# The last layer's residual kept in blocked feature order, beside its normed rows

## The reference

```python
h = rms_norm(x, g_norm1) * (1.0 + sc1) + sh1
...
mix = jnp.concatenate([attn, conv], axis=-1) @ w_out
x = x + gt1 * mix

h2 = rms_norm(x, g_norm2) * (1.0 + sc2) + sh2
x = x + gt2 * hier_moe(h2, ...)          # 32 experts, each token goes to 2 of them
return rms_norm(x, g_final)

# one expert on its rows
(silu(rows @ w_gate[e]) * (rows @ w_up[e])) @ w_down[e]
# w_gate, w_up: 1024 x 512 each, w_down: 512 x 1024; 2 MB each
```

## Time and profile before

| | |
|---|---|
| median of 3 runs | 1577.19 us (1577.14 to 1578.6) |
| the profiled execution's own time | 1580.41 us |
| its span (first to last instruction) | 1578.6 us |
| PE matmul busy | 1398.5 us, 89% |
| DVE busy | 680.4 us, 43% |
| ACT busy | 354.6 us, 22% |
| POOL busy | 110.9 us, 7% |
| moved by DMA | 338.08 MB, mean 214 GB/s |
| mean granted TensorE clock | 0.959 |

### The profile page before, as it was taken

One profiled execution on the slowest core, in us unless ns is written; L12 is line 12 of the kernel. 1 busy time (PEld: TensorE's weight loads), 2 busy tenths in 40 slices (PEclk: granted clock), 3 DMA queues, 4 the chain that ended last, 5 costly groups with the idle time before them and its releaser, 6 DMA issues.

```text
span 1578.6 us, 17570 instructions
## 1 busy us (share of the span) xinstructions
PE 1398.5 (89%) x6706; PEld 706.5 (45%) x6706; DVE 680.4 (43%) x1259; ACT 354.6 (22%) x776; POOL 110.9 (7%) x227
## 2 busy tenths in 40 slices
PE   4999999999999899999899978979996977868784
PEld 2444444555464444664644445455442333323331
DVE  4674114884366623322499775263121112111125
ACT  2434104562220243431400063110000000000001
POOL 3000000010100000001100000112000000000012
PEclk9999999999999999999999989989997989989896
DMA  9763315004276541003424123169999999999993
GB/s 340 277 222 107 103 57 125 2 1 160 91 254 218 184 160 54 1 1 107 152 88 160 54 107 158 57 235 393 413 414 412 415 415 417 413 414 419 416 395 157
DMA packets 97421, 338.08 MB, mean 214 GB/s; under 512 B 10343, under 2 KB 16280, under 8 KB 88760
## 3 DMA queue, kind: packets, MB, share of 16 engines
q1 hardware_dynamic: 83040, 307.24, 50.7%
q0 software_dynamic: 5664, 13.70, 3.1%
q10 hardware_dynamic: 8632, 15.99, 2.8%
HBM read 323.34 MB, written 17.24 MB: 216 GB/s over the span
## 4 chain that ended last, share of the span: by engine, by line
PE 65%; DMA 17%; DVE 11%; issue 3%; ACT 2%; SPq 1%; POOL 1%; DVEq 0%; ACTq 0%; POOLq 0%
PE bank L707 16%; PE score_banks L699 14%; DMA slots<-in_w_exp_up 12%; PE score_banks L1139 8%; PE bank L1166 4%; PE bank L881 3%; PE bank L683 3%; PE score_banks L707 2%; PE score_banks L1153 2%; DMA slots<-in_w_mod 2%; PE bank L981 2%; PE score_banks L972 2%; DVE bufD L1922 2%; PE score_banks L893 1%; DVE slots L1922 1%
## 5 line engine op out<-in xcount | busy, mean ns | idle before, releaser
L707 PE MATMUL bank<-slots 128*128 128x512 f32 x608 | 264.8, 593 | 2.6 <-PE bank L707 1.2
L699 PE MATMUL score_banks<-slots 128*128 128x512 f32 (+1 forms) x584 | 245.1, 578 | 6.6 <-ACTq L1298 4.0
L1139 PE MATMUL score_banks<-slots,norm_row 128*64 128x512 f32 (+1 forms) x672 | 151.2, 623 | 41.9 <-DMA slots<-in_w_exp_up 41.6
L707 PEld LDWEIGHTS bank<-slots 128*128 128x128 f32 x608 | 114.1, 190 | 144.8 <-issue 143.6
L699 PEld LDWEIGHTS score_banks<-slots 128*128 128x128 f32 x584 | 112.0, 194 | 132.9 <-issue 129.8
L2375 DVE TENSOR_TENSOR mix<-probsT,score_banks 128x256 f32<-128x256 f32 (+1 forms) x39 | 14.4, 370 | 290.2 <-ACT probsT L1586 290.0
L1166 PE MATMUL bank<-slots,mix 128*64 128x512 f32 (+1 forms) x864 | 116.9, 486 | 11.8 <-issue 9.9
L1586 ACT ACTIVATE probsT<-score_banks 128x256 f32<-128x256 f32 (+1 forms) x39 | 13.4, 342 | 446.2 <-PE score_banks L1139 387.4
L1139 PEld LDWEIGHTS score_banks<-slots,norm_row 128*64 128x64 f32 (+1 forms) x672 | 51.8, 146 | 135.6 <-issue 135.0
L707 PE MATMUL score_banks<-slots 128*128 128x512 f32 (+1 forms) x256 | 97.0, 534 | 0.3 <-PE score_banks L707 0.3
L1139 PE MATMUL score_banks<-slots,mix 128*32 128x256 f32 x896 | 61.7, 436 | 25.3 <-DMA slots<-in_w_exp_up 25.3
(11 more groups left out here) (345 smaller groups left out, 1636.8 us busy)
## 6 DMA issues: line engine op xcount, KB each, us to landing
slots<-in_w_exp_down SPq DMA_DIRECT2D x32, 2048.0 KB
slots<-in_w_exp_gate SPq DMA_DIRECT2D x32, 2048.0 KB, 28.6
slots<-in_w_exp_up SPq DMA_DIRECT2D x32, 2048.0 KB
slots<-in_w_in SPq DMA_DIRECT2D x16, 2048.0 KB, 8.7
slots<-in_w_mod SPq DMA_DIRECT2D x24, 1024.0 KB, 5.2
slots<-in_ada_w SPq DMA_DIRECT2D x18, 1024.0 KB, 6.3
slots<-in_w_out SPq DMA_DIRECT2D x6, 2048.0 KB, 7.8
slots<-in_ada_w SPq DMA_DIRECT2D x3, 2048.0 KB, 20.2
```

The lines of the kernel that those rows point to most:

```text
L699: last = mm(bank[:, cols], w[:, k, lo:lo + P], src[:, k, cols], start=(k == 0), stop=(k == kts - 1))
L707: last = mm(bank[:, 0:cols], src[:, k, t * P:(t + 1) * P], rhs(k), start=(k == 0), stop=(k == kts - 1))
L1139: last = mm(out, rows[:, k, :], e_gu[it.p][:, :, k, c * pc.ff:(c + 1) * pc.ff], start=(k == 0), stop=(k == KT - 1))
```

## The change

The last layer's residual leaves `x`. When the last gated result is added, the sum is written to `bufC`, in blocks (`residual(t)` is tile t of it, `by_block` reads natural order as blocks). The normed rows now go to `x`, so both sides of the norm are contiguous. Everything behind works on the residual in `bufC`: the transposes for the router, the squares, the additions of results, and the last norm, which writes `bufA` back in natural order.

`pick_rows` still multiplies `C_tok` by `onehot`. Since `C_tok` now holds the residual before the norm, `onehot` is multiplied by 1/rms of each token first. The store of the normed rows reads `x`. The third set's down matrix (experts 3, 6, 9, ...) goes to `x`, and so do the results gathered into `gathered[0]`. Nothing but the store reads the normed rows in `x`, so SP's wait for `rows_picked` goes.

```diff
+        def by_block(row):
+            return row.rearrange("p (q k) -> p k q", k=KT)
+        def residual(t, half=slice(0, D // KT)):
+            return bufC[:, t * D:(t + 1) * D].rearrange("p (k q) -> p k q", k=KT)[:, :, half]
...
-        e_down.append(bufC.rearrange("p (k n) -> p k n", k=FT))
+        e_down.append(x[:, :, :])
...
-        gathered = [tok(bufC), hT.rearrange("p b n -> p (b n)").rearrange("p (t n) -> p t n", t=TT)]
+        gathered = [x[:, :, :], hT.rearrange("p b n -> p (b n)").rearrange("p (t n) -> p t n", t=TT)]
...
-            return j % SUMS // 2, slice(j % 2 * W, (j % 2 + 1) * W)
+            return j % SUMS // 2, slice(j % 2 * W // KT, (j % 2 + 1) * W // KT)
...
-            sp.dma_start(xs.rearrange("(t p) d -> p t d", p=P), C_tok).then_inc(xs_out, 16)
+            sp.dma_start(xs.rearrange("(t p) d -> p t d", p=P), x[:, :, :]).then_inc(xs_out, 16)
             sp.wait_ge(logitsT_ready, 2)
             load_ahead(2, 1)
-            sp.wait_ge(rows_picked, 2)
             sp.wait_ge(xs_out, 16)
             load_ahead(2, 2)
...
-                    transposes(tr_banks, tr_filled, [every_8th(x[:, t, :], k + j) for j in range(4)])
+                    transposes(tr_banks, tr_filled, [C_tok[:, t, (k + j) * P:(k + j + 1) * P] for j in range(4)])
...
-                fn(bufC[:, t * D:(t + 1) * D], x[:, t, :], ACT.Square, accum_out=ss[:, t:t + 1]).then_inc(squares_ready, 1)
+                fn(x[:, t, :], C_tok[:, t, :], ACT.Square, accum_out=ss[:, t:t + 1]).then_inc(squares_ready, 1)
...
-                v.tensor_tensor(onehot.rearrange("p t (e s) -> p t e s", e=PICKED),
+                chain(v.tensor_tensor(onehot.rearrange("p t (e s) -> p t e s", e=PICKED),
...
+                v.tensor_tensor(onehot, onehot, ss[:, 0:TT].unsqueeze(2).to_broadcast([P, TT, PICKED * WIDE]), ALU.mult)\
+                    .then_inc(onehot_ready, 1)
...
-                rows, out = x[:, t, :], C_tok[:, t, :]
-                if by_expert_block:
-                    rows, out = rows.rearrange("p (q k) -> p k q", k=KT), out.rearrange("p (k q) -> p k q", k=KT)
+                rows, out = (C_tok[:, t, :], x[:, t, :]) if by_expert_block else (x[:, t, :], C_tok[:, t, :])
...
-                chain(v.tensor_tensor(xt, xt, mix[:, j, :], ALU.add))
+                if by_expert_block:
+                    out = residual(t, slice(u * W // KT, (u + 1) * W // KT))
+                    chain(v.tensor_tensor(out, by_block(xt), by_block(mix[:, j, :]), ALU.add))
+                else:
+                    chain(v.tensor_tensor(xt, xt, mix[:, j, :], ALU.add))
...
-                v.tensor_tensor(x[:, t, cols], bank[:, :], x[:, t, cols], ALU.add).then_inc(taken, 1)
+                v.tensor_tensor(residual(t, cols), by_block(bank[:, :]), residual(t, cols), ALU.add).then_inc(taken, 1)
...
-                    chain(v.scalar_tensor_tensor(out=x[:, t, :], in0=gathered[k][:, t, :], scalar=own_slot[:, k * TT + t, 3:4],
-                                                 in1=x[:, t, :], op0=ALU.mult, op1=ALU.add))
+                    chain(v.scalar_tensor_tensor(out=residual(t), in0=by_block(gathered[k][:, t, :]),
+                                                 scalar=own_slot[:, k * TT + t, 3:4], in1=residual(t), op0=ALU.mult, op1=ALU.add))
...
-                v.scalar_tensor_tensor(out=bufA[:, t * D:(t + 1) * D], in0=x[:, t, :], scalar=ss[:, t:t + 1],
-                                       in1=gate_row[:, :], op0=ALU.mult, op1=ALU.mult).then_inc(prod_ready, 1)
+                v.scalar_tensor_tensor(out=by_block(bufA[:, t * D:(t + 1) * D]), in0=residual(t), scalar=ss[:, t:t + 1],
+                                       in1=by_block(gate_row[:, :]), op0=ALU.mult, op1=ALU.mult).then_inc(prod_ready, 1)
```

More of the change, by code:

```diff
@@ L1285, in square @@
                 act.wait_ge(x_ready, need_x)
-                fn(C_tok[:, t, :], x[:, t, :], ACT.Square, accum_out=ss[:, col:col + 1]).then_inc(squares_ready, 1)
+                rows, unread = (x[:, t, :], C_tok[:, t, :]) if need_x <= 3 * TT else (C_tok[:, t, :], x[:, t, :])
+                fn(unread, rows, ACT.Square, accum_out=ss[:, col:col + 1]).then_inc(squares_ready, 1)
             def norm_tile(n, t):
@@ L1806, in route @@
                                              op0=ALU.mult, op1=ALU.add))
-                v.tensor_tensor(onehot.rearrange("p t (e s) -> p t e s", e=PICKED),
-                                slots_below.unsqueeze(1).unsqueeze(1).to_broadcast([P, TT, PICKED, WIDE]),
-                                rank_below.unsqueeze(3).to_broadcast([P, TT, PICKED, WIDE]), ALU.is_equal).then_inc(onehot_ready, 1)
+                chain(v.tensor_tensor(onehot.rearrange("p t (e s) -> p t e s", e=PICKED),
+                                      slots_below.unsqueeze(1).unsqueeze(1).to_broadcast([P, TT, PICKED, WIDE]),
+                                      rank_below.unsqueeze(3).to_broadcast([P, TT, PICKED, WIDE]), ALU.is_equal))
+                v.tensor_tensor(onehot, onehot, ss[:, 0:TT].unsqueeze(2).to_broadcast([P, TT, PICKED * WIDE]), ALU.mult)\
+                    .then_inc(onehot_ready, 1)
                 counts, count = bank[0:NE, n:n + NE], bank[0:NE, n + NE:n + NE + 1]
@@ L1995, in _, with residual_part @@
             ropes = [0]
-            def residual_part(u, t):
+            def residual_part(u, t, by_expert_block=False):
                 bank = dve_banks.take(dve)
@@ L2002, in residual_part, with residual_tile @@
                 xt = x[:, t, u * W:(u + 1) * W]
-                chain(v.tensor_tensor(xt, xt, mix[:, j, :], ALU.add))
-            def residual_tile(t):
-                residual_part(1, t)
+                if by_expert_block:
[3 more added lines that the diff above has]
+                    chain(v.tensor_tensor(xt, xt, mix[:, j, :], ALU.add))
+            def residual_tile(t, by_expert_block=False):
+                residual_part(1, t, by_expert_block)
                 dve.sem_inc(x_ready, 1)
@@ L2010, in residual_and_norm @@
                 for t in range(TT):
-                    residual_part(0, t)
-                residual_tile(0)
-                residual_tile(1)
+                    residual_part(0, t, by_expert_block)
+                residual_tile(0, by_expert_block)
+                residual_tile(1, by_expert_block)
                 scale_tile(0, 0, by_expert_block)
-                residual_tile(2)
+                residual_tile(2, by_expert_block)
                 scale_tile(1, 1, by_expert_block)
                 scale_tile(2, 2, by_expert_block)
-                residual_tile(3)
+                residual_tile(3, by_expert_block)
                 scale_tile(3, 3, by_expert_block)
```

## The result

The changed kernel takes 1585.78 us (median of 5 runs, 1585.34 to 1587.08); the kernel before takes 1577.19 beside it (5 runs, 1577.03 to 1578.6). The ratio is 1.0052, 95% interval 1.004 to 1.0063: **slower by 8.6 us**, between 6.3 and 9.9. The forecast was 1577.1, the range ended at 1582.5. The profiled execution took 1585.71 us (span 1584.0), against 1580.41 (1578.6).

A forecast was written before the change was run, and what follows sets the result against it. The prediction took the always-busy DMA queue to bound the expert part. 0.73 us from the multiply, -0.85 from the queue and 0 from strides gave -0.1: 1577.19 to 1577.1 us, range 1574.5 to 1582.5.

The forecast's parts named there:

- the 12 units: DVE operations at the end, per 1024 elements: 6 gathered results, 4 sums, 2 norms; upper bound 12 x 0.41 = +4.9 us.
- The early load: Third expert's down matrix on SP's queue: issued near 1043.0 instead of 1057.61, landing near 1053; queue gain -0.85 us.
- front and queue: Before the experts: 0.73 us later from the multiply by 1/rms, -0.85 from the DMA queue; net -0.1 us.
- the faster rival: DMA queue in the expert part: the whole down matrix leaves the bound part, gaining 4.3 us, 1572.9; chance 0.08.
- the queue's upper bound: Fourth expert's gate load on an empty queue: full start loss, no gathered rows passing meanwhile, +1.1 us.
- the narrow range: Whole kernel: the forecast's own range, 1575.2 to 1579.6 us, chance 0.70.
- the stride bound: DVE operations that become strided: at most 0.41 us more per 1024 elements, +4.9 us at the end; zero was taken.
- The multiply: `onehot` times 1/rms on DVE before picking: 0.69 us, moving PE until the first expert by 0.73 us.
- The scaling and the transposes: Last layer's scaling and PE's router transposes become contiguous: counted zero, at best -0.4 us for the transposes.
- the residual additions: Eight DVE additions that become strided: covered at either bound by waits for PE's banks, 4.7 us each.
- Every strided stream costs: DVE operations at the end: each 0.41 us longer per 1024 elements, +4.9 us, 1582.0; chance 0.16.
- a stride cost above my bound: Strided DVE operations: more than 0.41 us extra per 1024 elements; chance 0.03.

The follow-up runs named there:

- e1_probe: A kernel of its own, not the reference: VectorE operations at various steps, small POOL multiplies beside some; a contiguous 512-element addition takes 0.69 us.
- e3_end_straight: Changed kernel with gather additions and last norm reading and writing straight through, features mixed up: 1579.1 us, ratio 1.0005 to the kernel before.
- e9_natural_end: Changed kernel with the first eight sums putting the residual back in natural order, into the third expert's gate matrix: 1578.76 us, ratio 1.0005.

## Why the prediction was wrong, point by point

- **The step that failed** is "So they run at the pace that the strided one keeps, and the lower bound, which I take, is zero. The upper bound is the step from 750 to 1156, 0.41 us per 1024 elements." A strided operand is no floor that the slower two-input operations lie above; it adds to each element's time, about 0.75 ns here and 0.40 ns in the scaling with one input. Measured: 0.38 us per 512 and 0.77 per 1024 elements, nearly twice my upper bound. The rows held a better estimate: 1156 / 750 is a factor of 1.54, and by it 691 would have become 1065 ns and 1285 become 1980; measured 1075 (in `e1_probe`) and 2063. The sum over the 12 units would then have come to some +8.6 us by my estimate, the measured difference, but by luck: it counts 3.0 for the sums, which cost nothing, and nothing for POOL. Why the time grows as a factor is not shown. A price between two shapes should be carried over as a factor and as a difference, and the range should hold both.
- **Counting the units** was nearly right. Of 12, six (gathered results) cost 0.78 us each, 4.7. The four of sums cost nothing, as the only strided operand that stays on the path there is a bank in PSUM. The two of norms cost 1.5.
- **POOL was not in the sum.** 1.55 us come from POOL's steps, which are held by the norms beside them. The rows stood in the trace of before: 0.69 and 1.62 us were already the held ones, next to 0.19 and 0.72 for the same operations a moment earlier, beside additions that read a bank.
- **The early load** was issued at 1041.87 and landed by 1053, as described, and the next load started slowly (175 GB/s over 3 us, 137 predicted from before). The predicted net of front and queue, -0.1 us, was not resolved. `e3_end_straight` and `e9_natural_end`, which have the front of the change and the end of before, both give +0.05%, 0.8 us, with 0 within the interval. The lower ends of both intervals, -0.6 us, exclude the faster rival and its -4.3 us. Two sums of mine do not add up: rows that can't pass meanwhile cost 0.63 us once, so the queue's upper bound was +0.5 and not +1.1; and the top of the narrow range, 1579.6, holds half of the stride bound but nothing of the queue's.
- **The multiply** took 0.70 us, 0.69 predicted.
- **The scaling and the transposes** brought nothing, as predicted; the residual additions at 1.09 us are not seen in the time, as predicted: with them in place the kernels with a straight end are within 0.8 us of before.
- **The rival** "Every strided stream costs" had a chance of 0.16 and 1582.0 us, and its direction is what happened; the case that came true in size, a stride cost above my bound, had 0.03. It was wrong twice: in size (0.77 instead of 0.41) and in that not every stream costs, since PSUM's is free. By my own condition, slower than 0.2% from 0.27 us per 1024 on, the price decided alone. The Trainium skill's rule of 16-byte lines (SBUF — State Buffer, Door 1: The DMA port swizzle) was the better guide: two hits in a line are enough, which is a step of two floats (692 ns here), while a step of four costs the full price (1059). The same section's example, four float32 values as the step that is free, does not hold here. Its 8-byte lines for PSUM, a penalty that it states for matmuls, do not show for VectorE (691 ns with the bank in blocks).

The account, from the two profiles: +4.7 for gathered results, +0.3 up to the last sum (within what that piece varies by), +1.5 for the second pair of norms, +1.55 on POOL, -0.25 for the stores behind the norms: +7.8 us. The medians differ by 8.6 us, between 6.3 and 9.9. The 0.8 us between the two are as much as is left when the end is straight, but neither is told from zero, so that they are the front's is not shown.

## What to carry to other kernels

Before a buffer changes its layout, list every operation that reads or writes it, mark those on the chain that sets the end, and price each at one and a half times its duration if an SBUF operand is then at a step of four floats or more (measured here for float32, 512 and 1024 elements, steps of 4, 8 and 16: factors of 1.46 to 1.61). Cheap reordering is to be had where a wait covers it or where the operand is a PSUM bank, so turn the data there and keep the chain contiguous. And where a small POOL operation runs beside a long two-input VectorE operation, count it as long as the rest of that one.

## What the runs showed of the hardware that was not expected

- One strided float32 operand in SBUF, read or written, takes the addition of 512 elements from 0.69 to 1.07 us; three take it no further. With a step of 2 it still takes 0.69 us, with one of 4 it takes 1.06, and with 16 it takes 1.02.
- VectorE reads a PSUM bank in blocks at a step of 8 floats for nothing (691 ns either way).
- POOL's 128x2 multiply goes from 193 to 1040 ns on average beside contiguous scaled additions with two SBUF inputs, and stays at 194 beside additions that read a bank.
- At a granted clock of 1.00, picking matmuls with weights at a step of 8 floats took 0.25 us each instead of 0.12 (weight loads 336 instead of 192 ns); at 0.50 the weight loads were 338 and 334 ns.
